# Difference attention's norm products at the ends of turns, modulation steps out of the down products, last feed-forward blocks split before the last weights

## What is computed

```
# first stack, even layer (queries x, keys and values of x and context)
ya = window attention with sink(qa, ka, va)                 # "att A"
s  = q @ k.T / 8;  p = softmax(s)                           # two maps for each of 4 heads
yb = ((p[0] - lam * p[1]) @ v)                              # difference attention, "att B"
yb = rmsnorm(yb, g) * (1 - lam_init)                        # over the 128 columns of a head
y  = concat(ya, yb) * silu(gates);  x = x + gate * (y @ w_out)

# second stack, each layer
shift, scale, gate, ... = split(silu(c) @ mod_w + mod_b, 6) # modulation, depends on c alone
x = x + gate  * mixer(rmsnorm(x) * (1 + scale) + shift) @ w_out
x = x + gate2 * (silu(h @ wg) * (h @ wu)) @ wd              # feed-forward, width 2816
```

## Time and profile before

| What | Value |
|---|---|
| Median of 3 runs | 2376.01 us (2374.91 to 2379.13) |
| The profiled execution, its own time | 2372.06 us |
| Its span | 2370.3 us |
| Granted clock over the span | 0.994 |
| PE busy | 2278.4 us, 96% |
| PEld busy | 1722.5 us, 73% |
| DVE busy | 1301.3 us, 55% |
| ACT busy | 788.9 us, 33% |
| POOL busy | 331.9 us, 14% |

### The profile page before, as it was taken

One profiled execution on the slowest core, in us unless ns is written; L12 is line 12 of the kernel. 1 busy time (PEld: TensorE's weight loads), 2 busy tenths in 40 slices (PEclk: granted clock), 3 DMA queues, 4 the chain that ended last, 5 costly groups with the idle time before them and its releaser, 6 DMA issues.

```text
span 2370.3 us, 30353 instructions
## 1 busy us (share of the span) xinstructions
PE 2278.4 (96%) x11784; PEld 1722.5 (73%) x11784; DVE 1301.3 (55%) x2871; ACT 788.9 (33%) x1675; POOL 331.9 (14%) x333
## 2 busy tenths in 40 slices
PE   7999999989999999999999999999989999999997
PEld 5866576568645667787776888887767677888876
DVE  3565655655246654657767366666358844433333
ACT  4255103431112203623557122223433642222243
POOL 2200110001000112021200110003533002000154
PEclk9999999999999999999999999999999999999999
DMA  7200331002234363022310245554322102322321
GB/s 307 72 20 35 107 107 63 18 28 72 93 111 138 90 206 92 10 89 83 107 37 2 72 157 191 185 178 164 108 76 72 54 1 89 119 95 91 105 97 72
DMA packets 58267, 225.88 MB, mean 95 GB/s; under 512 B 20478, under 2 KB 21118, under 8 KB 41740
## 3 DMA queue, kind: packets, MB, share of 16 engines
q1 hardware_dynamic: 58124, 223.94, 28.2%
HBM read 221.83 MB, written 2.10 MB: 94 GB/s over the span
## 4 chain that ended last, share of the span: by engine, by line
PE 87%; DVE 5%; POOL 2%; ACT 2%; issue 1%; DMA 1%; SPq 1%; POOLq 0%; ACTq 0%; DVEq 0%
PE PS L86 82%; PE PS L91 5%; POOL WKr L103 1%; ACT WK L98 1%; DVE WK L108 1%; DMA GB<-in_ev_ada 1%; DVE WK L142 1%; SPq L162 1%; ACT WK L96 1%; POOL SM L103 0%; POOL Xr L103 0%; DVE X L103 0%; DVE ACC L115 0%; DVE WK L103 0%; ACT WKr L96 0%
## 5 line engine op out<-in xcount | busy, mean ns | idle before, releaser
L86 PE MATMUL PS<-Hr,GBr 128*128 128x512 f32 x1272 | 434.8, 393 | 2.2 <-ACT Hr L96 2.2
L86 PE MATMUL PS<-Hr,RINGr 128*128 128x512 f32 (+1 forms) x1048 | 405.6, 387 | 0.0
L96 ACT ACTIVATE WK<-PS 128x512 f32<-128x512 f32 (+2 forms) x391 | 189.1, 516 | 482.0 <-PE PS L86 290.2
L86 PE MATMUL PS<-H,RING 128*128 128x512 f32 (+1 forms) x928 | 336.3, 514 | 0.0
L115 DVE SCALAR_TENSOR_TENSOR ACC<-ADA,SM,ACC 128x256 f32<-128x256 f32 x608 | 297.1, 512 | 50.0 <-DMA ADA<-in_l_mod 30.8
L86 PEld LDWEIGHTS PS<-Hr,GBr 128*128 128x128 f32 x1272 | 237.8, 188 | 55.7 <-issue 3.4
L86 PEld LDWEIGHTS PS<-H,RING 128*128 128x128 f32 x928 | 172.0, 190 | 135.1 <-issue 126.9
L103 DVE TENSOR_TENSOR RINGr<-RING,GBr 128x1024 fp32r<-128x1024 f32 x148 | 182.5, 1271 | 145.5 <-ACT GBr L96 145.5
L86 PE MATMUL PS<-RING,GB 128*128 128x256 f32 x1152 | 252.6, 381 | 3.4 <-DVE GB L120 2.2
L86 PEld LDWEIGHTS PS<-RING,GB 128*128 128x128 f32 x1152 | 219.4, 191 | 34.7 <-issue 5.0
L86 PEld LDWEIGHTS PS<-Hr,RINGr 128*128 128x128 f32 (+1 forms) x1048 | 197.2, 188 | 40.6
(11 more groups left out here) (221 smaller groups left out, 2849.0 us busy)
## 6 DMA issues: line engine op xcount, KB each, us to landing
ADA<-in_l_mod SPq DMA_DIRECT2D x96, 512.0 KB, 3.8
RING<-in_l_gu SPq DMA_DIRECT2D x44, 1024.0 KB, 4.9
RING<-in_l_wd SPq DMA_DIRECT2D x24, 1024.0 KB, 4.9
RING<-in_ev_in SPq DMA_DIRECT2D x13, 1024.0 KB, 5.6
ADA<-in_od_ada SPq DMA_DIRECT2D x24, 512.0 KB, 3.6
RING<-in_od_in SPq DMA_DIRECT2D x11, 1024.0 KB, 6.1
RING<-in_l_in SPq DMA_DIRECT2D x10, 1024.0 KB, 4.9
RING<-in_l_out SPq DMA_DIRECT2D x8, 1024.0 KB, 5.3
```

The source lines that it names most:

```text
L86: self.last = self.eng.matmul(out, lhsT, rhs, start=start, stop=stop, skip_group_check=True)
L96: self.last = self.eng.activation(out, in_, func, bias=bias, scale=scale)
```

## The change

Four things are moved. No operation is added or taken away.

- **Att A:** one value tile in turn 0, one in turn 1 and two in turn 2, in place of two in turn 1 and two in turn 2.
- **Att B:** PE's two norm products stand at the end of turns u+4 and u+5, behind the value products and the gate part. Before, they stood inside turns u+5 and u+6. DVE has its part at the front of turns u+5 and u+6, ahead of gates and maxima.
- **Modulation:** the down product of layer 0 has no steps. The output projection of layer 0 has 3, 2, 1 and 0 steps behind its four tiles. The feed-forward of layer 1 has more of the steps among its up blocks.
- **Last blocks, in both layers:** ACT rounds blocks 39 to 43 together, ahead of the last weight chunk; DVE makes the lower halves of 40 to 43 ahead of that chunk too.

The pieces below are, in this order: the tables; PE in att B; PE, ACT and DVE in the down product, with DVE's `attention` between them; DVE in att B and in out l0; SP in out l0. POOL and ACT have `ada(OUT_STEPS[t])` at the same place in out l0.

```
-FFN_STEPS = {"l0f": (3, 3), "l1f": (1, 0)}
+FFN_STEPS = {"l0f": 3, "l1f": 1}
+OUT_STEPS = (3, 2, 1, 0)
...
+        VA_AT = {0: (0,), 1: (1,), 2: (2, 3)}
...
-            return [(u, step) for u in B_DONE for step in (0, 1) if i == u + 5 + step]
+            return [(u, step) for u in B_DONE for step in (0, 1) if i == u + 4 + step]
...
                 if 25 < i < 30:
                     out_early("ev_out", i - 26)
-
-            attention("B", sub_norms, at_end)
+                sub_norms(i)
+
+            attention("B", None, at_end)
...
                         chunk_done(FIRST[wd] + hh * 6 + cj)
-                        if hh == 0:
-                            ada(FFN_STEPS[st][1])
...
                             fz = hh * 22 + cj * 4 + z
-                            round_a(fz + 1)
+                            if fz < 38:
+                                round_a(fz + 1)
+                            elif fz == 38:
+                                for kept in range(39, 44):
+                                    round_a(kept)
...
                 for i in range(n + 6):
+                    if front is not None:
+                        front(i)
...
                         rest(i)
-                        if cj + hh * 6 < 11:
-                            rest(i + 1)
-                        if hh == 0:
-                            ada(FFN_STEPS[st][1])
-                    if hh:
-                        for z in range(40, 44):
+                        for z in range(40, 44) if hh and cj == 4 else ():
                             dve.wait_ge(act_value, ("ah", wd, z))
                             dve.tensor_tensor(AL_at(z), GB[:, z % 22 * 512:z % 22 * 512 + 512], AH_at(z), ALU.subtract)
                             dve.then_inc(dve_value, ("al", wd, z))
+                        if cj + hh * 6 < 11:
+                            rest(i + 1)
...
-                for u, step in diff_steps(i):
+                for u, step in diff_steps(i - 1):
...
-            attention("B", sub_norms)
+            attention("B", front=sub_norms)
...
+            def normed_with_steps(t):
+                norm_tile("l0f", t)
+                ada(OUT_STEPS[t])
...
             ada_until(ADA_AFTER["l0m", 5])
+            for n in OUT_STEPS:
+                ada(n)
             for j in range(4):
                 load()
```

More of the change, by code:

```diff
@@ L1175, in ffn @@
                     chunk_done(i)
-                    ada(FFN_STEPS[st][0])
+                    ada(FFN_STEPS[st])
                 ada_until(ADA_AFTER[st, 5])
@@ L1276, in values_a @@
             def values_a(i):
-                if 0 < i < 3:
-                    tm_split("ev", 2, 128, 128, "va", lambda t: copied("va", t, 0), VA_TILES[2 * i:2 * i + 2])
+                if i < 3:
+                    tm_split("ev", 2, 128, 128, "va", lambda t: copied("va", t, 0), VA_AT[i])
                     if i == 2:
@@ L1543, in tensor @@
             since(pe, "att S")
-            out_proj("l0_out", range(4), lambda k, t: None)
+            out_proj("l0_out", range(4), lambda k, t: None, lambda t: ada(OUT_STEPS[t]))
             cur.allowed |= {"l1m"}
@@ L1877, in values_a @@
             def values_a(i):
-                if i > 1:
-                    for t in VA_TILES[2 * i - 2:2 * i]:
-                        copy_out("va", t, 0, 128)
+                for t in VA_AT.get(i - 1, ()):
+                    copy_out("va", t, 0, 128)
             attention("A", values_a)
@@ L2395, in weigh, with attention @@
                         dve.then_inc(dve_probs, ("probs", tag, u))
-            def attention(tag, extra=None, behind=None):
+            def attention(tag, extra=None, behind=None, front=None):
                 units, n, lag = UNITS[tag], len(UNITS[tag]), LAG[tag]
                 for i in range(n + 6):
+                    if front is not None:
+                        front(i)
                     for t, s0, m in filled(tag, i):
@@ L2498, in ffn @@
                             dve.then_inc(dve_value, ("al", wd, z))
-                        if st == "l0f":
-                            rest(FIRST["l1_ki"])
+                        if cj + hh * 6 < 11:
+                            rest(i + 1)
+                    if hh and st == "l0f":
+                        rest(FIRST["l1_ki"])
                     for t in range(4):
@@ L2594, in wholes @@
             def wholes(i):
-                for t in VA_TILES[2 * i:2 * i + 2] if i else ():
+                for t in VA_AT.get(i, ()):
                     copy_out("va", t, 0, 128)
@@ L2885, in vector @@
             since(dve, "att S")
-            out_proj("l0_out", "l0m", range(4), ("c2",), lambda t: norm_tile("l0f", t), "l0_gu")
+            def normed_with_steps(t):
+                norm_tile("l0f", t)
+                ada(OUT_STEPS[t])
+            out_proj("l0_out", "l0m", range(4), ("c2",), normed_with_steps, "l0_gu")
             cur.allowed |= {"l1m"}
@@ L3052, in ffn @@
                     pool.then_inc(pool_value, ("al", wd, fz))
-                    if fz < 22 and (fz % 4 == 3 or fz == 21):
-                        ada(FFN_STEPS[st][1])
                 for t in range(4):
```

6 lines of the change are left out of this document (1 added, 5 removed).

## The result

The changed kernel takes 2351.72 us (median of 4 runs, 2350.11 to 2353.52); beside it the kernel before took 2375.46 (median of 4, 2372.75 to 2379.13). The ratio is 0.9899, with a 95% interval of 0.9882 to 0.9916. In the two profiled executions the span went from 2370.3 to 2351.4 us, 18.9 less; the medians differ by 23.7.

The account below looks back on a forecast made before the run. PE was taken to bound the kernel (96% of the span, DVE 55%). Terms -3.4 - 8.3 + 0.9 - 3.8 - 3.3 gave -17.9 us, 2354.2 from the profiled 2372.06, or 2358.1 as the median; range 2351 to 2366.

Parts of the forecast that it names:

- Att A, -3.4: Att A, PE's scores of unit 1: a value tile covers the 1.68 us wait; 3.4 us gained, bounds 1.7 to 3.6.
- with it the reason for the low clock: Att A, behind the 1.68 us wait: the 3.70 us stretch at clock 0.54 goes too, 1.70 us.
- Att B, -8.3: Att B: PE's waits go and a smaller one comes; 8.3 us gained, 4 or 10.5 as the other cases.
- The walk through turn 8: Att B, turn 8: PE ready at 418.1, DVE's chain done at 418.8, so a new wait of about 0.8 us.
- 3.37 us per period: Att B: six PE waits in the six turns of a head, 3.37 us, all go; three such periods.
- Out l0, +0.9: Output projection of layer 0: first up load 2.7 us later delays the last addition; 0.9 us lost, bounds 0 to 3.
- Down product, -3.8: Down product of layer 0: without steps the 2.15 us wait and 1.64 us of low clock go; 3.8 us gained.
- Last blocks, -3.3: Last blocks, both feed-forwards: 0.1 to 0.3 us replaces PE's wait of 1.8 to 2.0; 1.65 us each, 3.3 gained.
- The diagonal did not hold PE in full: Rival, att B: PE waits 2.3 us in place of 0.8 in wide turns; 5 us less gain, 2363; chance 0.2.
- POOL was held for 0.3 us: Rival, last blocks: POOL is blocked, PE held 1.0 us in each layer; 2360.1; chance 0.12.
- DVE did not become the pace: Rival, att B: diagonals and multiplications land on the scores' loop; +15 in place of -8.3, 2381.1; chance 0.03.
- The clock's rival: Rival, att A and down product: two low-clock stretches have another reason and stay, only idle time goes; 2361.4; chance 0.1.

## Why the prediction was right in sum and wrong in its terms

The four edits alone took 3.6, 12.8, 2.3 and 6.1 us off the medians beside them, 24.8 in sum against 23.7 together, so they hardly touch each other. That the span's change, -18.9 us, came within 1 us of the forecast is luck: errors of both signs cancelled, att B's 3.9 us too little against att A's 1.8 too much, out l0's 1.9 too kind and 1.35 in the up blocks that had not been counted. The medians, 23.7 us apart, are 5.8 beyond the forecast.

**Att A, -3.4.** The mechanism of the wait was right: the second scores start without one, and the tile covers it; 1.6 us. The step "with it the reason for the low clock" failed as a term. In the compared profiles the stage gained 1.58 us, just outside the bounds of 1.7 to 3.6. Of two executions of the changed kernel both lost 1.7 us behind the next waits, and of seven others with this edit one did. The price of the clock is not a number that one profile gives: over five profiles of the old order it is 5.1 us on average, between 0 and 8.5, and 0.6 over nine of the new. The stage itself was 276.2 us long on average over the five, and 270.7 over the seven new ones in which it is as in the changed kernel: 5.5 us in place of the 1.6 of the compared pair, whose profile of before had caught a mild case.

The granted clocks of the timed runs are a check with more executions, though rounded to 0.001. With this edit alone they average 0.9930 over ten runs, against 0.9919 over the 22 of the kernel before beside them: 2.7 us of clock. For the whole change they average 0.9932 over eight runs, 15.9 us lost against 19.3. So of the 23.7 us between the mean spans 3.5 are clock and some 20 are not, most of them idle time. In the compared pair the clock had gone the other way, from 14.2 to 16.9 us lost, and that is why the spans differ by less than the medians.

**Att B, -8.3; measured -12.24.** The walk through turn 8 was right: squares and spreads wait no more, and the new wait is the gate product's, 0.65 us against 0.8 forecast, for bank 7. What failed is the step "3.37 us per period": the brackets were added as if each were all that a wait costs, and the stage gained more than the bound of 10.5. The windows of one period before and after:

```profile
412.06:446.97 34.91, 31.55 (x172) 1.00 0.09 31
...
414.11:445.25 31.14, 30.52 (x172) 1.00 0.10 34
```

The same 172 instructions are 1.03 us less *busy*. Each product before a wait is drawn to its end (0.39 us, where the next would have started after 0.227), and that tail is time that the bracket does not count. Over all of att B idle time fell by 9.24 us (14.80 in 23 waits to 5.56 in 8), the stage by 12.24: 0.20 us for each wait that went. So this period gained 3.77 where 2.55 was forecast, 1.0 of it tails. Turns 23 and 24 gave 1.1 where 0.6 was counted: their waits are 0.88 and 0.54 now, in place of 1.57 and 0.93.

The Trainium skill (TensorE: Matmul & The Clock Gate, "Single matmul latency") puts the constant part of a single bf16 product's latency at 166 ns at the full clock. An estimate from that page's figure is that 15 waits would hide 2.5 us, against the 3.0 measured.

**Out l0, +0.9; measured +1.96 beside the apply's 0.8.** Every step of the chain was right and in order; the load's landing was mis-sized. It was issued 3.1 us later than before, shifted by what had been gained and by the apply (1333.46 against 1330.3), not 2.7, and took 5.8 us to ACT's start, not 4.9; the last modulation chunk had been issued 0.4 us ahead of it. DVE's lower half then ended 2.0 us too late for the last addition, in place of 0.7. What the prediction left out is the clock behind it: PE's wait at the last transposes grew from 1.59 to 2.87 us, and six of the seven profiles with that wait lose 3.4 us there. In four of them the up blocks are 255.1 to 255.4 us long in place of 254.1, so the late load costs about 1 us more than the table's row of out l0 says.

"Nothing in sum" for the apply was right: 0.8 us here, 0.8 less in the down product. The steps added to layer 1 cost nothing, 526.42 us against 526.55.

**Down product, -3.8.** Right in the compared pair: 2.15 us of wait and 1.71 of slow stretch. The wait is sure. The slow stretch stood behind it in three of the five profiles with that wait (the two of the kernel before differ in it) and in none of the nine without, so on average it was worth 1 us rather than 1.7. The 2.71 us at its start stayed, as forecast, and its cause was the one named.

**Last blocks, -3.3; measured -4.1.** Right in place and kind; 2.05 us each in place of 1.65. Block 20 found its weights: DVE began the last chunk at 1713.94 and PE had no wait at all there, so that neither the 0.1 to 0.3 us nor the tail of the old wait was paid.

The rule of the Trainium skill that was weighed there (SBUF — State Buffer, "Who interferes with whom") came true, only with the roles reversed. By it a vector operation with two SBUF inputs contends with GpSimd's reads for a shared port, and, as the page puts it for the vector engine's two-port modes, whoever issues first has the port for its whole instruction while the other blocks fully. POOL's block began 0.08 us before DVE's, and DVE's took 1.76 us in place of 0.6, ending 0.55 after POOL's. POOL's second, begun while DVE's first was still under way, took 0.3 us longer, and DVE's second again ended 0.54 behind it. The prediction had worked the rule out with DVE as the holder. Block 39 was 0.3 us late, and nobody waited for it.

**The rivals.** The diagonal did not hold PE in full (0.65, not 2.3); POOL was held for 0.3 us and PE not at all; DVE did not become the pace, though with its part behind the maxima, and PE's waits for the bank that come of it, the kernel was 16 us slower. The clock's rival ("another reason than the waits") was half right: a wait stands ahead of every slow stretch in att A, but the same wait has one behind it in some executions and none in others. Of the list of signs, the period (31.14 against 32.3), the load (3.1 against 2.7) and block 20 missed; the clock behind the second scores was 1.00, as named. PE's waits in att B sum to 5.6 us, under the bound of 8.

## What to carry to other kernels

Where a bracket's wait is removed, add the tail ahead of it (0.2 us here); with six short waits in a row that is a third more than the brackets say. When work is moved that leaves a result in a bank, move its reader with it: half of such an edit can leave nothing of the gain (att B 152.7 us beside its slow stretches, 153.5 with neither half and 141.3 with both). Price idle time from the profile, but the clock behind it only from several profiles, and from the granted clocks of the timed runs.

## What the runs showed of the hardware

- Behind a wait of 1.68 us PE's clock was at its full level in one execution, and at the lower one (1.2 GHz) for some 3.4, 14 and twice 17 us in four others, with PE busy for 14.00 of 14.00 and 17.17 of 17.20 us in two of them. What ends such a stretch stays open. Ten timed runs of one kernel, unchanged, took 2369.3 to 2382.4 us, and their granted clocks run from 0.995 for the fastest to 0.988 for the slowest. The Trainium skill (TensorE: Matmul & The Clock Gate, "What's actually happening") says that the number of products that a kernel runs at the low clock when it starts varies from run to run; here the same holds in the middle of a kernel.
- A slow stretch costs nothing where the engine would wait anyway: with up to 1.7 us lost behind layer 0's first up product the up blocks took 254.0 to 254.2 us in eight profiles, five with a loss of 1.4 to 1.7 us and three with next to none, and with 3.0 to 3.1 us lost 255.1 to 255.4 in four.
- Two engines subtracting from the same memory: a 128x512 block on DVE took 1.76 us while POOL was in one, 0.62 alone; POOL's took 1.62 and 1.29, 1.33 alone. The one that began second paid, for the rest of the other's block.
